# Sample value products placed behind the prompt's and the state space's steps in each turn of the cache stage on TensorE

## What is computed

```python
def fox_attend(q, c_q, q_pos, k, v, c_k, k_pos):        # 8 heads of 64
    s = einsum('bqhd,bkhd->bhqk', q, k) * ATTN_SCALE
    s = where(causal, s + (c_q - c_k), -inf)            # c: running sum of log forget values
    return einsum('bhqk,bkhd->bqhd', softmax(s), v)

# sample: per sequence, 32 pages of 128 rows from the paged cache, then its 8 new rows
k_all = concatenate([cache_k[layer, pages].reshape(4096, 8, 64), k_b])
v_all = concatenate([cache_v[layer, pages].reshape(4096, 8, 64), v_b])

# both: S5 state space, h[t] = lam_bar * h[t-1] + B u[t];  y = Re(C h) + d * u
# then: out = z * sigmoid(z @ w_glu + b_glu), z = gelu(y); mix, w_out, and a MoE of 64 experts, top 8
```

## Time and profile before

| | us |
|---|---|
| median of three runs | 1684.0 (1674.58 to 1685.24) |
| the profiled execution, its own time | 1683.99 |
| its span, first to last instruction | 1682.3 |
| mean granted TensorE clock | 0.937 of full speed |
| TensorE busy with matmuls | 1471.1 (87%) |

### The profile page before, as it was taken

How to read it: one execution, slowest core, us unless ns; L and a number is a source line. 1 busy time by engine, 2 the same in 40 slices (tenths; PEclk the granted TensorE clock), 3 DMA queues, 4 the chain that set the end, 5 groups by cost and what they waited for, 6 DMA issues and landing times. The chain is left out here.

```text
span 1682.3 us, 30837 instructions
## 1 busy us (share of the span) xinstructions
PE 1471.1 (87%) x10126; PEld 779.2 (46%) x10127; DVE 657.2 (39%) x1867; ACT 388.0 (23%) x1014; POOL 218.7 (13%) x292
## 2 busy tenths in 40 slices
PE   3999879999999999749887787876999999999967
PEld 2444546666677776424553333332333334444422
DVE  1323046777666766242352212222233333333323
ACT  2101135444444444310000111111111111111100
POOL 1000110004073320000001101111111111111100
PEclk9999869999999999979898889898999999999979
DMA  7112289998988989370007699999999999566267
GB/s 290 35 30 44 49 230 312 323 303 293 310 282 269 306 300 330 99 249 25 32 1 300 243 405 393 392 408 405 375 396 404 403 402 401 190 226 227 106 274 247
DMA packets 159292, 433.54 MB, mean 258 GB/s; under 512 B 48177, under 2 KB 50258, under 8 KB 132434
## 3 DMA queue, kind: packets, MB, share of 16 engines
q1 hardware_dynamic: 134144, 390.50, 63.7%
q0 software_dynamic: 14688, 38.82, 6.1%
q10 hardware_dynamic: 10354, 2.87, 0.9%
HBM read 409.41 MB, written 37.39 MB: 266 GB/s over the span
## 5 line engine op out<-in xcount | busy, mean ns | idle before, releaser
L2335 PE MATMUL ps_gu<-w_gu,mixT 128*32 128x512 f32 (+2 forms) x1664 | 357.1, 621 | 51.6 <-SPq L2130 50.7
L2335 PEld LDWEIGHTS ps_gu<-w_gu,mixT 128*32 128x32 f32 (+2 forms) x1664 | 123.7, 138 | 280.1 <-issue 266.8
L2352 PE MATMUL ps_y<-w_dn,aT_e 128*32 128x512 f32 (+2 forms) x832 | 175.9, 598 | 4.6 <-DVE aT_e L2277 2.4
L1352 PE MATMUL ps_kT<-ident,k_ring 128*128 128x128 f32 x1024 | 144.7, 284 | 17.0 <-DVE kT_grp L1006 9.4
L1352 PEld LDWEIGHTS ps_kT<-ident,k_ring 128*128 128x128 f32 x1024 | 116.2, 146 | 76.5 <-issue 47.6
L2275 DVE TENSOR_TENSOR act_in<-sil,ps_gu 128x256 f32<-128x256 f32 x48 | 20.2, 422 | 276.2 <-ACT sil L2219 276.2
L2174 POOL DMA_INDIRECT kT<-h_dram,idx x50 | 50.7, 1015 | 449.2 <-DVE idx L2251 449.2
L2219 ACT ACTIVATE sil<-ps_gu 128x256 f32<-128x256 f32 x48 | 18.4, 384 | 374.2 <-PE ps_gu L2335 374.2
L1006 DVE COPY kT_grp<-ps_kT 128x512 f32<-128x512 f32 x128 | 87.8, 686 | 42.3 <-PE ps_kT L1352 41.5
L2352 PEld LDWEIGHTS ps_y<-w_dn,aT_e 128*32 128x32 f32 (+2 forms) x832 | 55.5, 132 | 92.4 <-issue 84.1
L847 ACT COPY kT_grp<-ps_kT 128x512 f32<-128x512 f32 x128 | 75.1, 587 | 95.1 <-PE ps_kT L1352 95.1
(11 more groups left out here) (504 smaller groups left out, 1905.9 us busy)
## 6 DMA issues: line engine op xcount, KB each, us to landing
k_ring<-in_cache_k SPq DMA_DIRECT2D x256, 256.0 KB, 3.8
v_ring<-in_cache_v SPq DMA_DIRECT2D x256, 256.0 KB, 4.6
w_gu<-in_w_gate_e SPq DMA_DIRECT2D x64, 1024.0 KB, 7.6
w_gu<-in_w_up_e SPq DMA_DIRECT2D x64, 1024.0 KB, 10.8
w_dn<-in_w_down_e SPq DMA_DIRECT2D x64, 1024.0 KB, 8.7
w_gu<-parts_dram SPq DMA_DIRECT2D x6, 2048.0 KB, 19.1
w_in<-in_w_in SPq DMA_DIRECT2D x8, 1028.0 KB, 21.8
w_gu<-in_w_out SPq DMA_DIRECT2D x1, 4096.0 KB, 18.7
```

The lines of the kernel that those rows point to most:

```text
L1352: last = pe.transpose(ps_kT[:, j % 2, e * PAGE:(e + 1) * PAGE], k_places[n % RING][:, e * DA + j * P:e * DA + (j + 1) * P], m.ident[:, :])
L2335: last = pe.matmul(ps_gu[at, :].rearrange("p (g n) -> p g n", g=2), xgT[:, u, k, at], w_gu[:, place, :, k, :].rearrange("p s g n -> p (s g ...
L2352: last = pe.matmul(ps_y[at, n, :], aT[:, j, at], w_dn[:, place, j, n * 512:(n + 1) * 512].rearrange("p s n -> p (s n)"), start=(j == 0), s ...
```

## The change

On TensorE `rows_transposed` and `past_values` move from ahead of `out_transpose` to behind `p_transposes`, so that a turn's value products come last, after the prompt's and the state space's steps. On VectorE `sample_placed` moves behind `maximum` and `inverse`. Nothing is added or removed, and the lists of ScalarE, SyncE and GpSimd stay as they are.

```diff
@@ VectorE, each turn
                     if turn < N_GRP:
                         kT_copy(turn, 3)
-                    if n_out >= GPS and n_out % GPS == 0:
-                        sample_placed(n_out // GPS - 1)
                     if turn >= 4 and turn % 2 == 0 and turn // 2 - 2 < UNITS // 2:
                         placed(turn // 2 - 2)
                     if u < UNITS:
                         maximum(u)
                     if 1 <= u <= UNITS:
                         inverse(u - 1)
+                    if n_out >= GPS and n_out % GPS == 0:
+                        sample_placed(n_out // GPS - 1)
                     if 1 <= u <= UNITS:
                         transposed(u - 1)
@@ TensorE, each turn
                         k_transposes(turn, 3)
-                    if n_val > GPS and (n_val - 1) % GPS == 0:
-                        rows_transposed((n_val - 1) // GPS - 1)
-                    if 0 <= n_val < N_GRP:
-                        past_values(n_val)
                     if turn >= 4 and turn % 2 == 0 and turn // 2 - 2 < UNITS // 2:
                         out_transpose(turn // 2 - 2)
...
                     if 1 <= u <= UNITS:
                         p_transposes(u - 1)
+                    if n_val > GPS and (n_val - 1) % GPS == 0:
+                        rows_transposed((n_val - 1) // GPS - 1)
+                    if 0 <= n_val < N_GRP:
+                        past_values(n_val)
                     if turn == SKIP_AT - 2:
                         last_states()
```

## The result

The changed kernel took 1695.03 us, the median of 11 runs (1683.99 to 1697.82); the kernel before took 1677.09 beside it (11 runs, 1668.58 to 1685.24). The ratio is 1.0091, with a 95% interval of 1.0064 to 1.0118: some 15 us slower. Its profiled execution took 1689.83 us, with a span of 1688.1 and a mean granted clock of 0.939 (before: 1683.99, 1682.3 and 0.937). So the pair of profiles differs by 5.8 us, and the medians by 17.9, some three times that.

The account below looks back on a forecast made before the run. TensorE was taken to set the turns, so only its waits of 23.4 us could be won. Gains of 3.4 and 2.4 less a loss of 6.7 made 0.9 us slower on 1683.99: forecast 1685 us, range 1675 to 1694.

Parts of the forecast that it names:

- The gain in the prompt's turns: Prompt's turns: VectorE gets scores 1.08 us earlier, shrinking six TensorE waits for key copies; gain 3.4 us, bounds 0 to 3.9.
- The wait for mixT: Turns 11, 19 to 59 except 35: TensorE's wait of 1.06 us falls to about 0.66; gain 2.4 us.
- SyncE's list: Turns 43, 49, 55: later value loads delay y writes, then key copies and `skip`; loss 5.4 plus 1.3, 6.7 us.
- What is not reached: VectorE waits of 5.5 us in turns 36, 37, 46, 52, 58 and ScalarE's 5.6 in turn 63 stay.
- The first rival: New waits in turns 45, 51, 57 make the clock fall once or twice more: 1690 or 1695 us; chance 0.27.
- Gains alone: SyncE's delay of the y writes is absorbed, loss near 0, time 1678 us; chance 0.15.
- the fall removed: Shifted waits let the clock hold in turn 37: minus 5 us, 1680, or 1673 with gains alone; chance 0.10.
- Pages too late: Bunched value loads push keys behind their use; 0.4 us in each of 64 turns, 26 us, 1710; chance 0.03.

Follow-up runs that it names:

- second pair of profiles: Both kernels run again unaltered: the changed kernel 1690.09 us, ratio 1.0086; the kernel before 1680.76 us, ratio 1.0013 of itself.
- ssm_only: Against the kernel before, values late only in turns from 33 on, with `sample_placed` in its old place: 1692.42 us, ratio 1.0094.
- y_first: Changed kernel with SyncE's y writes ahead of the value pages: 1688.26 us, ratio 1.0057 to the kernel before.
- pool_later: Changed kernel with GpSimd's first state space step also waiting for the turn's value products: 1682.72 us, ratio 1.0038 to the kernel before.
- the last experiment: Changed kernel, y writes first, GpSimd's powers and outputs held back, values in old place in turns 33 to 37: 1668.77 us, 0.9939 to the kernel before.

## Why the prediction was right and wrong

Taken as a ratio, the forecast was 1.0006, and 1.0091 was measured: still within 1%, so the class that was given 0.92 holds, narrowly. The range ended at 1694 on a basis of 1684, a ratio of 1.0060, and the measured interval lies wholly above it. The median, 1695.03, is 1 us outside.

**The gain in the prompt's turns: right, its size a little high.** 3.4 us of the waits for VectorE were to go, and 3.5 went (3.9 to 0.4). The prompt's part shortened by 1.7 in the first profile and 2.8 in the second, since a cost was not seen: VectorE copies `mixT` (L1074) for the value product of the prompt (L1428) behind the same turn's key copy, and 1.08 us of value products used to stand between. TensorE waits 0.39 there in turns 8, 16 and 24, and 0.96 in turn 32 (0.47 before).

**The wait for mixT: right, mis-sized.** The term was 2.4 us; 2.1 went, of which three turns gave some 0.2 each and three 0.49.

**SyncE's list: right mechanism, too large.** The term was 5.4 + 1.3. The added waits of TensorE in turns 45, 51 and 57 are 1.05, 0.34 and 0.46, thus 1.9 where 2.4, 1.7 and 1.3 stood. In the second pair of profiles they are 1.06, 0.79 and 0.92, thus 2.8. ScalarE's waits for y_scr grew by 1.62, 0.29 and 0.66 instead of 3.0, 1.7 and 1.5. That turns stretched by VectorE's longer steps gave slack to the y writes is likely, and not shown by a run. The undo of this part was worth some 5 us in the medians; of that, 2.5 are in turn 63 (5.8 to 3.3), which the change had not made longer by more than 0.2.

**The step that failed** is the one under "What is not reached": that VectorE's waits of turns 36, 37, 46, 52 and 58 come from scans and from `skip`, "which start behind the key copies of their turn and not behind the values", and so stay as they were. That they start behind the key copies is right. How long they take was assumed to be fixed, and the working never followed what the moved steps release on GpSimd. `w_tr` and `y_mm` come one step of 1.08 us earlier in the turn, and GpSimd's reads fall upon VectorE's scans and additions. The waits for VectorE then grew: from 0.42 to 1.27 in turn 36, from 2.01 to 2.44 in 37, from 0.42 to 1.92 in 46 and to 1.67 in 52, and new ones came in turns that had none (39, 40, 42, 43, 48, 49 and 54). The medians price it at 8 us for the scans and 7 us for the outputs. The cause is shown, since one wait on GpSimd takes it away with TensorE's order untouched; the prices are rough, since the waits seen in the profiles fell by 5.5 and 3.4 us. The 5.5 us that the prediction counted here were partly chance, too: in the second profile of before they are 3.4.

The Trainium skill, in SBUF — State Buffer, section "Who interferes with whom", says that a VectorE instruction with two inputs in SBUF contends with a GpSimd instruction that reads SBUF. The Trainium skill, in SBUF — State Buffer, section "SBUF: two separate sides", says of this pair that whichever starts first holds the shared ports for its whole instruction while the other blocks fully. Neither section names scans. This case's trace fits a lock of that kind. GpSimd ran instructions of 1.06, 1.06 and 1.28 us in turn 39 (L799 twice, L802), and of the eight scans five took 0.26 to 0.29 and the other three 1.09, 1.09 and 1.31. Each of the three began 0.11 to 0.12 us after an instruction of GpSimd and ended some 0.15 us after that instruction's end. That page would have pointed to the direction of the result beforehand.

**The first rival, one more fall of the clock, came about in another place.** Its place was wrong: turns 45 and 51 kept the clock, with waits of 1.05 and 1.28. Turn 37 lost it. Five profiles have the wait of 2.01 to 2.02 us in turn 37 with a wait of 0.42 in turn 36 ahead of it, two of them of the kernel before, and one of the five has the fall. Six profiles with the values late in these turns have waits of 1.14 to 1.30 in turn 36 and 2.44 in turn 37, and all six have it. `ssm_only` fell in turns 36, 46 and 52, `y_first` also in 46, `pool_later` also in 42. Stretches of turn 37 in the changed kernel, columns as in the earlier trace rows:

```profile
493.00:498.00 5.00, 3.67 (x23) 3.68 (x23) 4.13 (x10) 1.21 (x4) 2.94 (x3) 0.75 0.67 224
498.00:503.00 5.00, 5.00 (x50) 4.45 (x50) 0.28 (x2) 0.99 (x3) 0.00 (x0) 0.57 0.40 141
```

The shares of 0.75 and 0.57 in these two stretches make 2.5 + 4.3 = 6.8 us at the lower clock, where the kernel before had 10.2. The price of a fall went with this. Turn 37 with a full clock took 9.16 us behind a wait of 0.84 (`ssm_only`), and 13.98 behind 2.44 in the changed kernel: 4.8 more, of which 1.6 are the longer wait and 3.2 the fall's. The foretold 5 us hold for the long falls only (4.4 and 0.3 in the kernel before).

So the fall that was an accident before came in every profile, and others joined now and then. This is also why the first pair of profiles understates the loss: the one of before held a fall as well, and a dearer one. The second pair differs by 14.9 us (1687.04 and 1672.17).

**Gains alone, the fall removed:** neither happened in the changed kernel. Both did in the profile of the last experiment, once the costs had been taken away; 0.9939 is 10 us, more than the 6 us that the gains alone were thought to be worth. Not all of it belongs to the move: the y writes' new place took 2 to 3 us off the wait of turn 63 wherever it was tried, and neither it nor GpSimd's waits were tried with the values in their old place throughout. **Pages too late:** fell. TensorE waits for no key or value page in the changed kernel.

**What stays open.** The split of the 15 us between longer VectorE steps and falls of the clock is known in the profiles only, not over all runs, since runs without a profile show one mean clock and none by turn. A version with the waits of turns 36 and 37 shortened, and all else as in the changed kernel, was not run.

## What to carry to other kernels

When a step moves on the engine that bounds, follow each semaphore that it raises to every engine, also to those far from being the bottleneck: what they start earlier can lengthen the work beside it. Compare the mean duration of the same instructions before and after, since a step that grew from 325 to 530 ns points to the cause at once, while a view of waits only names the victim. Take a second profile of the kernel before the change, too: here it differed from the first by 11.8 us, twice what the first pair of profiles showed between the kernels.

## What the hardware showed that was not expected

- A wait added on an engine that is not the bound made the program 8 us faster than the changed kernel, and a second one 7 us more, by the medians. VectorE's scan of 128x64 takes 265 ns alone and up to 1314 beside GpSimd's elementwise work on 128x512; its addition on 128x256 takes 0.42 alone and 1.27 beside it. GpSimd seems to be held, too: in turn 38 two instructions of L811 took 2.55 us where the first began 0.32 us into an addition of VectorE (L1213) and beside the next (L1214), which both kept their 0.42; before, they took 2.08.
- The same wait of 2.01 or 2.02 us ahead of the same transposes of turn 37 was followed by a granted clock of 0.50 (1.2 GHz) in one profile, and by 1.00 in four others. With some 1.2 and then 2.44 us in two successive turns it fell in six executions of six. Waits of 1.30 (turn 42), 1.68 (turn 52) and 1.92 (turn 46) were followed by a fall in some executions and not in others. In each case the clock fell within 2 us of the end of the wait, while TensorE was working again. The Trainium skill, in TensorE: Matmul & The Clock Gate, section "Why this matters for your kernels", says of a loop whose next products follow at once that VectorE's copy out of PSUM doesn't break the warmth of TensorE. Here TensorE had to wait for VectorE's copies of keys out of PSUM, and the clock did fall behind such waits, so its sentence can't be carried over to them.
- A fall did not always cost the same. It took 1.6 us in turn 42 of `pool_later` (9.18 us against 7.56 in the changed kernel) and 1.7 in turn 36 of `ssm_only` (9.21 against 7.53), 3.2 in turns 46 and 52 of `ssm_only` (13.41 against 10.24, 13.19 against 9.99), and 4.4 to 4.8 in turn 37 of the kernel before (14.83 against 10.39) and turn 46 of `y_first` (15.05 against 10.24).
